# Attention on cached keys and values in 32-column strips of the TensorE array

## The reference

```python
k_ext = jnp.concatenate([k_past, k_new], axis=1)      # 256 (or 128) cached keys and 8 new ones, of the SAME batch row
s = jnp.einsum('bqhd,bqjhd->bqhj', q, k_ext[:, idx]) * HEAD_DIM ** -0.5   # idx: dilated window
s = jnp.where(valid, s, -1e30)
p = jnp.exp(s - max(s)); o = einsum(p, v_ext[:, idx]) / sum(p)
# the three groups' outputs are merged by a softmax over their log-sum-exps
```

## Time and profile before

| what | us |
|---|---|
| median of 3 runs | 1313.48 |
| lowest and highest | 1313.40, 1315.09 |
| span of the profiled execution | 1312.0 |
| PE busy | 1269.2 (97%) |
| DVE busy | 727.9 (55%) |
| ACT busy | 487.1 (37%) |
| share of PE in the chain of work that ended last | 92% |

### The profile page before, as it was taken

How to read it: one execution, slowest core, us unless ns; L and a number is a source line. 1 busy time by engine, 2 the same in 40 slices (tenths; PEclk the granted TensorE clock), 3 DMA queues, 4 the chain that set the end, 5 groups by cost and what they waited for, 6 DMA issues and landing times.

```text
span 1312.0 us, 22213 instructions
## 1 busy us (share of the span) xinstructions
PE 1269.2 (97%) x9313; PEld 1223.8 (93%) x9313; DVE 727.9 (55%) x1212; ACT 487.1 (37%) x713; POOL 167.0 (13%) x255
## 2 busy tenths in 40 slices
PE   7899999999999999998999999999999999999996
PEld 6898998998899789998999999999999999999996
DVE  4973383283374348883333344788735886368821
ACT  4444444343443348774222234422222223122231
POOL 1271601601601100001000000000010001000021
PEclk9899999999999999999999999999999999999998
DMA  7382532522523112225323222232222223222321
GB/s 207 64 209 59 145 93 77 146 77 70 148 74 95 42 49 67 79 57 141 88 81 88 79 73 78 77 87 80 80 85 80 80 80 85 80 85 84 88 64 45
DMA packets 180436, 117.13 MB, mean 89 GB/s; under 512 B 6844, under 2 KB 172890, under 8 KB 180345
## 3 DMA queue, kind: packets, MB, share of 16 engines
q1 hardware_dynamic: 168944, 87.34, 23.5%
q0 software_dynamic: 11392, 28.79, 8.0%
q10 hardware_dynamic: 28, 0.01, 0.0%
HBM read 107.66 MB, written 8.45 MB: 89 GB/s over the span
## 4 chain that ended last, share of the span: by engine, by line
PE 92%; DVE 3%; ACT 2%; issue 1%; DMA 1%; POOL 0%; SPq 0%; ACTq 0%; POOLq 0%; DVEq 0%
PE ps L503 76%; PE ps L666 4%; PE ps L511 2%; PE ps L625 2%; PE ps L735 1%; PE ps L611 1%; PE ps L600 1%; DMA x_tok<-in_x_prompt 1%; PE ps L643 1%; PE ps L588 1%; DVE prob L1268 1%; DVE hn L1201 1%; ACT w_hi L862 0%; PE ps L791 0%; PE ps L808 0%
## 5 line engine op out<-in xcount | busy, mean ns | idle before, releaser
L503 PE MATMUL ps<-h_hi,w_hi 128*128 128x288 f32 x1824 | 404.0, 303 | 7.5 <-DVE h_lo L1204 3.9
L503 PE MATMUL ps<-h_hi,w_lo 128*128 128x288 f32 x1824 | 392.5, 297 | 0.0
L503 PE MATMUL ps<-h_lo,w_hi 128*128 128x288 f32 x1824 | 391.9, 297 | 0.0
L1168 DVE TENSOR_TENSOR w_lo<-w_raw,w_hi 128x1024 fp32r<-128x1024 f32 (+1 forms) x164 | 196.0, 1195 | 282.3 <-ACT w_hi L862 282.2
L862 ACT ACTIVATE w_hi<-w_raw 128x1024 fp32r<-128x1024 f32 (+1 forms) x164 | 170.3, 1038 | 445.3 <-PE ps L503 438.3
L503 PEld LDWEIGHTS ps<-h_hi,w_hi 128*128 128x128 f32 x1824 | 296.5, 190 | 12.4 <-issue 4.3
L503 PEld LDWEIGHTS ps<-h_lo,w_hi 128*128 128x128 f32 x1824 | 295.4, 190 | 0.0
L503 PEld LDWEIGHTS ps<-h_hi,w_lo 128*128 128x128 f32 x1824 | 295.3, 190 | 0.0
L1243 DVE RECIPROCAL qk_ri<-qk_rt 128x576 f32<-128x576 f32 x24 | 90.0, 3750 | 26.6 <-ACT qk_rt L941 26.6
L467 POOL DMA_DIRECT2D out<-f_row x12 | 6.2, 515 | 624.7 <-ACT f_row L1139 624.7
L503 PE MATMUL ps<-g_hi,w_hi 128*128 128x288 f32 x384 | 83.0, 297 | 1.6 <-DVE g_lo L1505 1.6
(11 more groups left out here) (281 smaller groups left out, 1781.6 us busy)
## 6 DMA issues: line engine op xcount, KB each, us to landing
w_raw<-in_w_in SPq DMA_DIRECT2D x68, 512.0 KB, 3.9
w_raw<-in_w_up SPq DMA_DIRECT2D x48, 512.0 KB, 3.9
w_raw<-in_w_down SPq DMA_DIRECT2D x24, 512.0 KB, 3.9
vc<-in_cache_v_g POOLq DMA_DIRECT2D x12, 512.0 KB, 6.2
kc<-in_cache_k_g POOLq DMA_DIRECT2D x48, 128.0 KB, 3.1
w_raw<-in_w_br_a SPq DMA_DIRECT2D x8, 512.0 KB, 3.9
w_raw<-in_w_out SPq DMA_DIRECT2D x8, 512.0 KB, 3.9
x_tok<-in_x_prompt SPq DMA_DIRECT2D x4, 512.0 KB, 9.7
```

The costliest lines, as they stand in the source:

```text
L503: last = mm(ps[p][:, 512 * h:512 * h + HALF], w[:, p, k, :], x[:, k, HALF * h:HALF * (h + 1)], start=(k == 0 and x is x_hi and w is w_hi), ...
L1168: TT(w_lo[:, u % NSPL, 0:nkt[u], :], w_raw[:, u % NRAW, 0:nkt[u], :], w_hi[:, u % NSPL, 0:nkt[u], :], ALU.subtract).then_inc(lo_ready, 1)
```

## The change: what it does

The eight batch rows are laid out in two slots of four: row b = 4s + j goes to slot s and strip j, and a strip is 32 columns of the array and 32 partitions of the PSUM tile. In strip j, columns 8s to 8s+7 hold the queries of row 4s + j, and 16 of the 32 columns stay zero. Score and value matmuls have a stationary operand of 32 columns, and the four strips' matmuls of one kind stand behind one another. `kcT` has six slots in place of two: six batch rows are transposed before the first score matmul. The result's rows lie on 128 partitions (64 of them in use), so masks, exponential and normalisation take all 128 rows, the transposes of P0 and O0 have 128 columns, the new keys' scores take two 128-column matmuls a group in place of one with 64, and `p_new` has 384 columns in place of 192, with its matmuls first.

```diff
-            q_dia = sb("q_dia", [P, NG, NB * (NS + NT)], at=m)
-            p_dia = sb("p_dia", [P, 4, NB * (NS + NT)], at=m)
-            p_new = sb("p_new", [NS, NG * NS], at=m)
-            NKC = 8
+            q_dia = sb("q_dia", [P, NG, DIA], at=m)
+            p_dia = sb("p_dia", [P, 4, DIA], at=m)
+            p_new = sb("p_new", [NS, NG * P], at=m)
+            NKC, NKT = 8, 6
-            kcT = sb("kcT", [P, 2, 4 * P], at=m)
+            kcT = sb("kcT", [P, NKT, 4 * P], at=m)
...
+        def strip(row, s, j):
+
+            return row[:, s * P + j * STRIP:s * P + (j + 1) * STRIP]
...
             def sample_scores(hp):
                 taken(pe, 9 * hp + 7)
-                for b in range(NB + 1):
-                    if b < NB:
+                for s in range(SLOTS):
+                    for b in (range(0, NKT), range(NKT, NB))[s]:
                         cached_keys_T(hp, b)
-                    if b == 0:
+                    if s == 0:
                         pe.wait_ge(q_dia_rdy, hp + 1)
-                        continue
-                    n = hp * NB + b - 1
-                    pe.wait_ge(kcT_rdy[n % 2], n // 2 + 1)
+                    n = hp * NB + 4 * s + 3
+                    pe.wait_ge(kcT_rdy[0], (n + 1) // 2)
+                    pe.wait_ge(kcT_rdy[1], (n + 1) // 2)
                     for g, c0, cn in ((0, 0, P), (1, P, 2 * P), (2, 3 * P, P)):
-                        last = mm(ps[2][0:NS, c0:c0 + cn], q_dia[:, g, (b - 1) * NS:b * NS], kcT[:, n % 2, c0:c0 + cn],
-                                  start=(b == 1 and g == 0), stop=(b == NB), skip_group_check=True)
-                    last.then_inc(kcT_used, 1)
+                        for j in range(4):
+                            last = mm(ps[2][j * STRIP:(j + 1) * STRIP, c0:c0 + cn], strip(q_dia[:, g, :], s, j),
+                                      kcT[:, (4 * s + j) % NKT, c0:c0 + cn],
+                                      start=(s == 0 and g == 0), stop=(s == SLOTS - 1), skip_group_check=True)
+                    last.then_inc(kcT_used, 4)
                 for g in range(NG):
-                    last = mm(ps[2][0:NS, 512 + g * NS:512 + (g + 1) * NS], qT[:, g, SEQ:TOK], kT[:, g, SEQ:TOK],
-                              start=True, stop=True)
+                    for s in range(SLOTS):
+                        last = mm(ps[2][:, 512 + g * NS:512 + (g + 1) * NS], q_dia[:, g, s * P:(s + 1) * P], kT[:, g, SEQ:TOK],
+                                  start=(s == 0), stop=(s == SLOTS - 1))
...
                     for n in range(4):
-                        tr(ps[TRN][:, n * NS:(n + 1) * NS], pr[0:NS, n * P:(n + 1) * P], ident[0:NS, 0:NS])
+                        tr(ps[TRN][:, n * P:(n + 1) * P], pr[:, n * P:(n + 1) * P], ident)
                     for g in range(NG):
-                        last = tr(ps[TRN][0:NS, 512 + g * NS:512 + (g + 1) * NS],
-                                  pr[0:NS, 512 + g * NS:512 + (g + 1) * NS], ident[0:NS, 0:NS])
+                        last = tr(ps[TRN][0:NS, 512 + g * P:512 + (g + 1) * P],
+                                  pr[:, 512 + g * NS:512 + (g + 1) * NS], ident)
...
-                    srcs = [(p_dia[:, n, b * NS:(b + 1) * NS], vc[:, b, n, :]) for b in range(NB) for n in range(4)]
-                    srcs += [(p_new[:, g * NS:(g + 1) * NS], v_tok[0:NS, 4, g, :]) for g in range(NG)]
+                    srcs = [(p_new[:, g * P:(g + 1) * P], v_tok[0:NS, 4, g, :]) for g in range(NG)]
                 for n, (p_, v_) in enumerate(srcs):
-                    last = mm(o_bank(hp, i), p_, v_, start=(n == 0), stop=(n == len(srcs) - 1))
+                    last = mm(o_bank(hp, i), p_, v_, start=(n == 0), stop=(n == len(srcs) - 1), skip_group_check=(i == 0))
+                if i == 0:
+                    for s in range(SLOTS):
+                        for n in range(4):
+                            for j in range(4):
+                                last = mm(o_bank(hp, 0)[j * STRIP:(j + 1) * STRIP, :], strip(p_dia[:, n, :], s, j),
+                                          vc[:, 4 * s + j, n, :], start=False, stop=(s == SLOTS - 1 and n == 3),
+                                          skip_group_check=True)
...
-                if n >= 2:
-                    act.wait_ge(kcT_used, n - 1)
-                A(kcT[:, n % 2, :], key_banks(hp)[:, 512 * (b % 2):512 * (b % 2) + 512], ACT.Copy).then_inc(kcT_rdy[n % 2], 1)
+                if hp or b >= NKT:
+                    act.wait_ge(kcT_used, NB * hp + 4 * (b // NKT))
+                A(kcT[:, b % NKT, :], key_banks(hp)[:, 512 * (b % 2):512 * (b % 2) + 512], ACT.Copy).then_inc(kcT_rdy[n % 2], 1)
```

More of the change, by code:

```diff
@@ L35 @@
 C_N = C_SM + 4 * P + NG * NS
+STRIP, SLOTS = 32, 2
+DIA = SLOTS * P + NT * SLOTS
 V_CW, V_CB, V_BA, V_BX, V_LAM, V_N1, V_N2, V_SC, V_H0 = 0, 4, 5, 6, 7, 8, 9, 10, 34
@@ L301, in diag, with strips, by_batch @@
         def diag(row):
-            return row.rearrange("p (b n) -> p b n", n=NS + NT)[:, :, 0:NT]
+            slots = row.rearrange("p (s n) -> p s n", n=P + NT)[:, :, 0:P]
+            return slots.rearrange("p s (j n) -> p s j n", n=STRIP)[:, :, :, 0:NT]
+        def strip(row, s, j):
+            return row[:, s * P + j * STRIP:s * P + (j + 1) * STRIP]
+        def strips(ap):
+            used = ap.rearrange("p (j n) -> p j n", n=STRIP)[:, :, 0:SLOTS * NT]
+            return used.rearrange("p j (s t) -> p s j t", t=NT)
+        def by_batch(ap):
+            return ap.rearrange("p (s j t) -> p s j t", s=SLOTS, t=NT)
         def key_banks(hp):
@@ L319, in o_bank, with out_src @@
         def o_bank(hp, i):
-            return ps[TRN][:, 6 * P:7 * P] if i == 4 else out_banks(hp)[0:P if i else NS, 0:HD]
+            return ps[TRN][:, 6 * P:7 * P] if i == 4 else out_banks(hp)[:, 0:HD]
         def oT_bank(hp, i):
-            return ps[TRN][:, 7 * P:8 * P] if i == 4 else out_banks(hp)[:, 512:512 + (P if i else NS)]
+            return ps[TRN][:, 7 * P:8 * P] if i == 4 else out_banks(hp)[:, 512:512 + P]
         def out_cols(buf, hp, i):
-            return in_time(buf[:, hp, 0:SEQ])[:, :, i - 1] if i else buf[:, hp, SEQ:TOK]
+            return in_time(buf[:, hp, 0:SEQ])[:, :, i - 1] if i else by_batch(buf[:, hp, SEQ:TOK])
+        def out_src(hp, i):
+            return oT_bank(hp, i) if i else strips(oT_bank(hp, i))
         def by_class(ap):
@@ L673, in out_T @@
                     pe.wait_ge(at_ready, e)
-                n = P if i else NS
-                tr(oT_bank(hp, i), o_sb[0:n, e % 2, :], ident[0:n, 0:n]).then_inc(at_ps, 1)
+                tr(oT_bank(hp, i), o_sb[:, e % 2, :], ident).then_inc(at_ps, 1)
             def attend(hp, step):
@@ L954, in exps @@
                 act.wait_ge(mx_ready, e + 1)
-                rows, n = (P, 6 * P) if i else (NS, 4 * P + NG * NS)
-                pr = prob[0:rows, e % 2, 0:n]
-                A(pr, pr, ACT.Exp, bias=stat[0:rows, e % 4, 2:3], accum_out=stat[0:rows, e % 4, 3:4]).then_inc(p_ready, 1)
+                pr = prob[:, e % 2, 0:6 * P if i else 4 * P + NG * NS]
+                A(pr, pr, ACT.Exp, bias=stat[:, e % 4, 2:3], accum_out=stat[:, e % 4, 3:4]).then_inc(p_ready, 1)
             def take_probs_T(hp, i):
@@ L968, in take_probs_T @@
                     for n in range(4):
-                        src = ps[TRN][:, n * NS:(n + 1) * NS]
-                        A(diag(p_dia[:, n, :]), src.rearrange("p (b t) -> p b t", b=NB), ACT.Copy)
-                    A(p_new[:, :], ps[TRN][0:NS, 512:512 + NG * NS], ACT.Copy).then_inc(pT_ready, 1)
+                        A(diag(p_dia[:, n, :]), strips(ps[TRN][:, n * P:(n + 1) * P]), ACT.Copy)
+                    A(p_new[:, :], ps[TRN][0:NS, 512:512 + NG * P], ACT.Copy).then_inc(pT_ready, 1)
             def out_hi(hp, i):
@@ L975, in out_hi @@
                 act.wait_ge(at_ps, e + 1)
-                A(out_cols(att_hi, hp, i), oT_bank(hp, i), ACT.Copy).then_inc(at_hi_rdy, 1)
+                A(out_cols(att_hi, hp, i), out_src(hp, i), ACT.Copy).then_inc(at_hi_rdy, 1)
             def take_cached_T(hp, b):
@@ L1262, in mask_max @@
                 st = stat[:, e % 4, :]
+                rows = P
                 if i:
-                    rows, n0, n1, m0, m1 = P, 4 * P, 2 * P, C_PM + (3 - r) * P, C_PM + 7 * P
+                    n0, n1, m0, m1 = 4 * P, 2 * P, C_PM + (3 - r) * P, C_PM + 7 * P
                 else:
-                    rows, n0, n1, m0, m1 = NS, 4 * P, NG * NS, C_SM, C_SM + 4 * P
+                    n0, n1, m0, m1 = 4 * P, NG * NS, C_SM, C_SM + 4 * P
                 for w, (s0, n, m) in enumerate(((0, n0, m0), (512, n1, m1))):
@@ L1276, in normed @@
                 e = hp * 5 + i
-                rows = P if i else NS
+                rows = P
                 st = stat[0:rows, e % 4, :]
@@ L1288, in out_lo @@
                 dve.wait_ge(at_hi_rdy, hp * 5 + i + 1)
[L1289 removed]
+                TT(out_cols(att_lo, hp, i), out_src(hp, i), out_cols(att_hi, hp, i), ALU.subtract).then_inc(at_ready, 1)
```

(6 more changed lines are left out.)

6 lines of the change are left out of this document (3 added, 3 removed).

## The result

The changed kernel takes 1274.7 us (median; 1270.35 to 1276.05) against 1314.12 before: a ratio of 0.9696, with a 95% interval of 0.9676 to 0.9715. Of the cases named beforehand the one with all four strips at once (1277.2) came true. The profiled execution of the changed kernel has a span of 1268.6 us, 43.4 under that of before.

The account below looks back on a forecast made before the run. TensorE was taken to bound the kernel; 2.26 + 0.3 - 0.34 + 3.31 - 0.05 = 5.48 us less a head, 21.9 for four, gave a span of 1290.1 and a median of 1291.6 us, range 1276 to 1312.

Parts of the forecast that it names:

- all four strips at once: Rival for scores and V0: 0.028 to 0.030 us a unit, 3.6 us more saved a head, 1277.2 us; chance 0.16.
- What bounds the kernel: Whole kernel: TensorE is 92% of the chain that ended last; the change reworks 84.5 us over four heads.
- The pace of a strip record: Scores and V0: 0.058 us a record in strips, between bounds of 0.111 (serial) and 0.028 (all four at once).
- The estimate from the Trainium skill: Strip matmuls: 0.047 us a unit, from 2.38 times for three column tiles; time some 5 us below the forecast.
- The keys stage: First transpose of cached keys to first prompt scores: 10.95 us instead of 13.21, 2.26 us less a head.
- Mask, P0, V0's surroundings: Per head: mask wait 0.3 us less, P0 0.34 more, V0 3.31 less, O0 0.05 more; `p_new`'s longer copy hidden.
- The serial rival: Scores and V0: strips one after another at 0.111 us, 1.35 us a head slower, 1318.9 us; chance 0.20.
- Sum for a head: All stages the change touches: 5.48 us less a head, 21.9 us for four.

Follow-up runs that it names:

- n3: n2 with the new keys' scores laid into strips as well; median 1256.97 us, 0.9582 of before, head's period 92.12 us.
- e2: Changed kernel with V0's order altered to two matmuls (four records) of one strip in a row; 1.96 us for the 64 records, period 95.24 us.
- e6: Changed kernel with all strip matmuls of scores and values sent to strip 0; 1317.65 us against 1314.03 before, a head 105.53 us.
- e1: Changed kernel with V0's order altered to four matmuls (eight records) of one strip in a row; 4.26 us instead of 1.88, period 97.55 us.
- e3: Changed kernel with V0's order altered so two strips take turns, then the other two; 2.42 us for the 64 records, period 95.70 us.
- e5: Changed kernel with V0's order altered to eight matmuls (sixteen records) of one strip in a row; 5.89 us, period 99.18 us.
- c1: The changed kernel unaltered, run again for comparison on the same chip; median 1275.95 us, 0.9705 of before, head's period 95.17 us.
- n1: Changed kernel with all eight batch rows transposed before the first score block; median 1271.51 us, 0.9678 of before, period 94.67 us.
- n2: n1 with two more PSUM banks for the transposes; median 1262.67 us, 0.9623 of before, period 92.79 us.
- e4: Changed kernel with cached keys transposed four rows and four instead of six and two; 1280.22 us timed once, period 96.05 us.

## Why the prediction was wrong, point by point

- **What bounds the kernel, and that the stage is PE's: right.** The 9.14 us by which the two stages shrank came off the period in full (9.48).
- **The pace of a strip record: this is the step that failed.** 0.058 was taken, 0.0268 was measured. Two reasons stood behind it. The first, that no pair of load and matmul had been seen below 0.057, read a limit into rows in which the moving operand's 64 columns (half of the 0.109 us of 128; in n3 one strip's 64-column records start 0.056 apart) already explained the pace; they said nothing about issue. The second, that the second record of a strip holds up the next strip, is refuted by the changed kernel's own rows (four strips start within 0.03 us) and by e2: even four records of one strip in a row leave the others at work. The mis-sized term is 128 units x (0.058 - 0.0268) = 4.0 us a head, 16 us in all, which is nearly the whole miss of 17 us. What the runs showed in its place: four strips work at once, each at its old pace of 0.109 us a record. The rival "all at once" had the right price and was given 0.16; its mechanism is now known.
- The estimate from the Trainium skill ("TensorE: Matmul & The Clock Gate", Part 3), 0.047 from its 2.38 times for three tiles, was nearer but still too high (the time it gives lies 5.8 us below the forecast, 512 x 0.0114, where the prediction said some 5); its 4 ns for each further tile is the better guide, since four records started some 7 ns apart here. Measured, four strips give 0.109 / 0.0268 = 4.07 times.
- **The keys stage: right but for the pace.** First scores expected 3.84 us after the first transpose, measured 3.98 (the idle time of 0.97 us that the prediction gives for it is 1.05 by its own starts, 3.71 less 24 x 0.111, and 1.19 when measured the same way); the distance from the first score block's end to the second's start 1.88, measured 1.87; L652 1.34 plus a switch, measured 1.39 (its records start 0.112 apart from the second on, as expected); with the right pace for strips S1 was expected at 9.15 (10.95 less twice 0.90), measured 9.25. The 10.95 doesn't quite add up from its terms, which give 10.88 (9.44 + 0.1 + 1.34): 0.3 us in all.
- **Mask, P0, V0's surroundings: right.** From S1 to P0 2.43 us against 2.80, 0.37 less where 0.3 stood; P0 0.82 against 0.9 expected; V0 2.74, where the rival's numbers add up to 2.82. `p_new`'s longer copy takes 0.49 us, as expected (0.33 + 0.16), and ends at 117.75, 0.28 before V0 starts: hidden.
- **The serial rival:** its sign is confirmed by e6, its price (1.35 us a head) was 0.83. The pace it took, 0.111, is 0.109, a matter of 0.26 us; the rest is spread over steps of a tenth.
- **Sum for a head.** 9.1 was worked out for "all at once", 9.5 measured, 36.3 and 38 us for four. 1.3 us below the range is within what the unchanged stages differ by.

## What to carry to other kernels

Where several small float32 products have stationary operands that fit in 32 columns, giving each a strip of its own and laying the strips in turn can cut the array's time to a quarter (0.0268 for 0.109 us a record here, at 128 moving columns); the narrower operand alone gives nothing (e6). Keep runs on one strip to four records, which is two float32 matmuls. Once the matmuls were four times faster they no longer covered the copies out of PSUM: price each copy again, and give the transposes as many banks as are idle in that stage.

## What was not expected of the hardware

- A strip takes four records before it holds up the others (e1, e2, e3, e5: 4.26, 1.96, 2.42 and 5.89 us for the same 64 records).
- The unchanged last stage takes either 486.13 or 481.00 us, with nothing between: 486.1 in the profiles of before, c1, n1, n2, e2, e4 and e6, 481.0 in those of the changed kernel, n3, e1, e3 and e5, at a granted clock of 1.00 in the four shown here and above. One kernel (as changed) shows both. The difference lies in two stretches of the stage, in which the same 288-column records start every 0.130 us in the short form and every 0.1333 in the long one; between these stretches both have 0.1333. In one of the two stretches 26 us of the changed kernel hold 203 records where c1 has 197 (windows below). Its cause is open; it must be left out when profiles are compared by their spans.

```profile
732.74:1218.87 486.13, 484.49 (x3645) 481.40 (x3644) 318.11 (x623) 138.80 (x170) 11.96 (x24) 1.00 0.28 81
```

```profile
718.15:1199.15 481.00, 479.22 (x3644) 476.14 (x3643) 318.01 (x623) 138.85 (x170) 11.99 (x24) 1.00 0.28 82
```

The first row is c1's, the second n3's. The two windows of 26 us, of the changed kernel and of c1:

```profile
841.33:867.33 26.00, 26.00 (x203) 26.00 (x201) 22.07 (x49) 6.79 (x8) 0.00 (x0) 1.00 0.28 83
```

```profile
844.11:870.11 26.00, 26.00 (x197) 26.00 (x196) 21.47 (x48) 6.79 (x8) 0.00 (x0) 1.00 0.28 81
```
